# The low part of each group's second U block made by GpSimd between its row gathers, in the last phase of a PEER expert layer

## The reference, cut to what matters

```
def expert_block(args):
    xb, eb, gb = args
    h = jnp.einsum('td,ted->te', xb.astype(f32), u[eb].astype(f32))
    a = jax.nn.gelu(h, approximate=False) * gb
    return jnp.einsum('te,ted->td', a, v[eb].astype(f32))
```

## Time and profile before

| what | value |
|---|---|
| median of 3 runs | 3098.43 us |
| lowest and highest run | 3095.93 and 3102.11 us |
| span of the profiled execution | 3101.7 us |
| TensorE busy in it | 85% of the span |
| VectorE busy in it | 74% of the span |
| GpSimd busy in it | 52% of the span |

### The profile page before, as it was taken

One profiled execution on the slowest core, in us unless ns is written; L12 is line 12 of the kernel. 1 busy time (PEld: TensorE's weight loads), 2 busy tenths in 40 slices (PEclk: granted clock), 3 DMA queues, 4 the chain that ended last, 5 costly groups with the idle time before them and its releaser, 6 DMA issues.

```text
span 3101.7 us, 40708 instructions
## 1 busy us (share of the span) xinstructions
PE 2646.0 (85%) x14892; PEld 2060.6 (66%) x14892; DVE 2307.6 (74%) x4892; ACT 1052.2 (34%) x1650; POOL 1611.6 (52%) x1187
## 2 busy tenths in 40 slices
PE   7998688889997566663667999999999999999996
PEld 5888577777776455551445767777777777777775
DVE  4520666655999899983767778887777777879999
ACT  4321433433454577760112222222222322222322
POOL 0001001112887555564666666766666767666674
PEclk9988799999998788886888999999999999999998
DMA  4231412221210599999999999999999999999995
GB/s 130 95 103 56 141 44 86 86 83 62 76 52 29 173 320 296 298 322 346 383 390 385 381 391 382 396 393 394 387 395 365 396 407 409 394 394 345 367 377 213
DMA packets 309647, 832.90 MB, mean 269 GB/s; under 512 B 26096, under 2 KB 114608, under 8 KB 309456
## 3 DMA queue, kind: packets, MB, share of 16 engines
q0 software_dynamic: 150864, 548.60, 46.1%
q1 hardware_dynamic: 158592, 281.78, 25.6%
HBM read 771.40 MB, written 58.88 MB: 268 GB/s over the span
## 4 chain that ended last, share of the span: by engine, by line
PE 15%; DVE 13%; DMA 11%; POOL 9%; issue 6%; ACT 0%; DVEq 0%; ACTq 0%; POOLq 0%
DMA e_u_row<-in_u,ids 11%; POOL hold L1975 6%; DVE e_u_row L2213 3%; POOL e_u_row L1966 3%; PE psum L2051 2%; PE psum L2052 2%; PE psum L2053 2%; PE psum L2018 2%; PE psum L2019 2%; PE psum L2020 2%; PE psum L2066 2%; DVE e_y L2203 2%; DVE e_u_row L2222 1%; DVE e_vl L2171 1%; DVE hold L2222 1%
## 5 line engine op out<-in xcount | busy, mean ns | idle before, releaser
L1966 POOL DMA_INDIRECT e_u_row<-in_u,ids x384 | 484.4, 1261 | 339.0 <-DVE ids L2213 234.7
L2213 DVE CUSTOM_DVE_ANT_0 e_u_row<-e_u_row,hold 128x1024 f32<-128x1024 f32 x384 | 467.9, 1223 | 255.5 <-DMA e_u_row<-in_u,ids 228.4
L2051 PE MATMUL psum<-e_vh,e_ah 128*128 128x512 f32 x1024 | 421.5, 412 | 98.1 <-DVE e_y L2203 78.5
L1975 POOL DMA_INDIRECT hold<-in_v,ids x376 | 436.4, 1161 | 131.4 <-issue 109.2
L2052 PE MATMUL psum<-e_vl,e_ah 128*128 128x512 f32 x1024 | 410.1, 401 | 0.0
L2053 PE MATMUL psum<-e_vh,e_al 128*128 128x512 f32 x1024 | 407.9, 398 | 0.0
L2018 PE MATMUL psum<-x1d,e_uh 128*128 128x512 f32 x864 | 341.3, 395 | 0.0
L2019 PE MATMUL psum<-x1d,e_uh 128*128 128x512 f32 x864 | 337.3, 390 | 0.0
L2020 PE MATMUL psum<-x1d,e_ul 128*128 128x512 f32 x864 | 336.3, 389 | 0.0
L2051 PEld LDWEIGHTS psum<-e_vh,e_ah 128*128 128x128 f32 x1024 | 198.1, 193 | 204.0 <-DVE e_y L2203 103.7
L2203 DVE TENSOR_TENSOR e_y<-e_y,psum 128x512 f32<-128x512 f32 x464 | 298.9, 679 | 10.4 <-PE psum L2053 9.2
(11 more groups left out here) (406 smaller groups left out, 5673.1 us busy)
## 6 DMA issues: line engine op xcount, KB each, us to landing
e_vr<-in_v SPq DMA_DIRECT2D x128, 512.0 KB
e_ur<-in_uT SPq DMA_DIRECT2D x108, 512.0 KB
s_G<-g_tile SPq DMA_DIRECT2D x8, 4096.0 KB, 26.5
e_g<-s_G SPq DMA_DIRECT2D x64, 512.0 KB
ids<-in_w_ch SPq DMA_DIRECT2D x17, 512.0 KB, 4.1
s_ch<-p_out POOLq DMA_DIRECT2D x16, 512.0 KB, 4.4
hold<-in_wq SPq DMA_DIRECT2D x16, 512.0 KB, 8.9
hold<-in_v,ids POOLq DMA_INDIRECT x476
```

The lines of the kernel that those rows point to most:

```text
L1966: pool.indirect_dma_start(out=u_ring[n % U_RING][:], out_offset=None, in_=io["u"], in_offset=bass.IndirectOffsetOnAxis(ap=id_u[:, s, k:k + ...
L1975: pool.indirect_dma_start(out=v_ring[m % V_RING], out_offset=None, in_=io["v"], in_offset=bass.IndirectOffsetOnAxis(ap=id_v[:, t:t + 1], a ...
L2051: nc.tensor.matmul(acc, ah[s][j][:, r], vh[s][j][:, c], start=(first and j == 0), stop=False)
L2213: nc.vector.tensor_tensor_reduce(row, row, xs[:, s, :], 1.0, 0.0, ALU.mult, ALU.add, hs[:, s, k:k + 1]).then_inc(dotted, 1)
```

## The change

In groups 53 to 62 the subtraction that makes `e_ul1` for the next group, `split_u(g + 1, 1)`, is taken out of DVE's order. GpSimd does the same subtraction, on the same buffers and with the same semaphores, at places between its gathers: before the first gather that waits for a row of slot 4 or later of group g. That makes ten subtractions, for groups 54 to 63. The block for j = 0 stays on DVE, as do both blocks in the phases before.

```
+                def split_u_low(g):
+                    pool.wait_ge(u_hi[1], g - SHORT + 1)
+                    nc.gpsimd.tensor_tensor(ul[1][:], ur[1][:], uh[1][:].bitcast(F32), ALU.subtract).then_inc(u_lo[1], 1)
+
+                s_at = {n: g + c / U_SLOTS for (g, c), ns in sums.items() for n in ns}
+                split_next = KEEP + 1
                 for n in range(U_RING - 1, P):
+                    while split_next < NG and n >= S_RING and s_at[n - S_RING] >= split_next - 0.5:
+                        split_u_low(split_next)
+                        split_next += 1
                     gather_last(n)
+                for g in range(split_next, NG):
+                    split_u_low(g)
...
                     dot_rows(g, 5)
-                    if SHORT <= g + 1 < NG:
+                    if SHORT <= g + 1 <= KEEP:
                         split_u(g + 1, 1)
```

## The result

The changed kernel takes 3104.94 us (median of 14 runs, 3098.98 to 3118.0), the kernel before 3098.47 us beside it (14 runs). The ratio is 1.0029, with a 95% interval of 1.0019 to 1.0040: 9 us slower, 6 to 12. The ratio is not that of the two medians, which lie 6.5 us apart, inside this interval. The profiled execution took 3103.53 us, with a span of 3101.9.

What follows compares the result with a forecast made beforehand. DVE, without idle time in the last phase, was taken as the bound; 4 x 1.03 - 0.23 + 5 x 0.67 = +7.2 us on 3098.4 gave 3105.6 us, with 80% between 3099 and 3111.5.

Steps and rivals of the forecast that it cites:

- What bounds the kernel: Last phase: DVE is busy 25.00 of 25.00 us, so removing ten subtraction slots of 1.14 us saves 11.4 us.
- The exclusion: POOL operations reading SBUF and DVE operations with two SBUF operands exclude each other for their whole length, about 2.3 us.
- The two deductions: Amounts taken off DVE's stall behind POOL's subtraction: 0.13 us at `split_a`, 0.19 us at a sum.
- POOL works beside DVE: Rival, last phase: DVE only loses its ten slots, -11.4 us, or 3087.0; chance 0.07.
- The size of the stall: Last phase: each POOL subtraction costs DVE 2.3 us, less what falls beside a PSUM addition, less 0.13 to 0.19.
- The groups with two rows in slot 4: Groups 53 to 57: POOL gets through ahead of `split_a`, DVE loses 2.17 us, net +1.03 in four of them.
- Group 53: Two PSUM additions in a row there; the stall behind them was put at 0.91 us, net -0.23.
- the five groups with one row: Groups 58 to 62: POOL starts at the PSUM addition (+0.37) or before a sum (+0.97); middle +0.67 each.
- The Trainium skill's floor: POOL's subtraction at about 2.5 cycles per two-input element, 2.13 us; by it the forecast would be 3103.9.
- Only beside the additions from PSUM: Rival, last phase: POOL gets through only beside PSUM additions, +3.1 us, or 3101.5; chance 0.28.
- What the stall makes late next: Last phase: PE's idle time in a group grows, while DVE stays at 25.00 of 25.
- What costs nothing: Last phase: POOL's low part is ready at W + 5.3 to 5.9 against W + 6.6; the ring covers later gathers.

Runs made afterwards that it cites:

- eight columns: Changed kernel, but POOL subtracts only the first 8 of 1024 columns at the same place, leaving part of the result out; 3087.53 us, ratio 0.9967.
- copy on top: Kernel before, DVE keeping its subtractions, plus POOL copies of a 128x1024 block into a spare buffer at the changed kernel's places; 3102.95 us, ratio 1.0019.
- pairs alone: Kernel before, with DVE's four additions from PSUM made as two pairs from group 54 on; 3098.06 us, ratio 0.9999.
- two halves: Changed kernel with additions from PSUM as two pairs and POOL's subtraction cut in two, each half beside a pair; 3096.87 us, ratio 1.0001.
- a half each: Against the changed kernel, POOL subtracts only 512 columns, beside a pair of PSUM additions; DVE does the rest in the old place; 3098.77 us, ratio 0.9997.
- fastest complete kernel: Changed kernel with POOL's subtraction halved beside paired PSUM additions, and SP loading gates ahead of `e_ur1` from group 53 on; 3095.02 us, ratio 0.9982.

## Why the prediction was right, and where it was not

The forecast was 3105.6 us, +7.2; measured were 3104.9 (+6.5 by the medians), +9.0 by the ratio (6 to 12), and +9.7 in the profiled phase.

- **What bounds the kernel**: right. Eleven microseconds taken from DVE come out as 10 (eight columns).
- **The exclusion**: right, and shown from both sides: the same work on top of everything costs 18 us of lengthened rows, the same place without the work costs nothing. The two deductions, 0.13 and 0.19 us, hold to 0.01 us in the rows above. The rival that POOL works beside DVE is refuted.
- **The size of the stall**: the term was a little too large. Forecast were 18.6 us of stall (7.2 and the 11.4 saved); the ten rows lose 16.9. The groups with two rows in slot 4 were taken for 2.17 each behind `split_a`; of those four it was so in two (2.14), and in two POOL got through only at the addition (1.54). Group 53 lost 0.95 (0.91 forecast), the five groups with one row 1.58 to 1.93 (1.81). POOL's length is 2.39 us where it is let through at once, as the earlier trace rows had it. The Trainium skill's floor (GPSIMD Engine Reference, Instruction dispatch), by which I had estimated 2.13, is 0.26 below that.
- **Only beside the additions from PSUM**: this rival describes eight of the ten groups, but not its price of +3.1. It has 14.5 us of stall where 16.9 were lost: two groups lose at `split_a`, and in two more POOL starts 0.3 us after the addition and the sum loses 1.9. And it has no late gelu.
- **What the stall makes late next**: this step failed. The prediction had TensorE idle for longer, at no price, and DVE at 25.00 of 25.00. Instead a stall ahead of an addition from PSUM stops TensorE, in three groups its clock falls, gelu is late there, and DVE stands idle for 3.5 us more than before in the phase. In the two groups with the same stall and the same wait of TensorE gelu is late only where the clock fell. The length of TensorE's waits does not order the rest: in "copy on top" it waits 21.6 us for DVE's additions and DVE 1.2 for gelu, in "eight columns" 9.0 and 2.3. But leaving out "eight columns" and the wait at the phase's start, every wait for gelu of over 0.4 us in these kernels (17) ends 6 to 10 us behind the end of a stretch at the lower clock. Not every such stretch makes gelu late: the kernel before has one and no late gelu, "pairs alone" four and one late gelu. For the other two waits of the changed kernel (0.69 and 1.71 us), where TensorE also stood still for longer (5.51 and 3.65 us), the shares of the clock and of the stop stay open.
- **What costs nothing**: right for the changed kernel; there DVE waits neither for rows nor for gates. The margin is small, as two halves and a half each show, where a later signal makes the gates late.

The too large stall (1.7 us) and the missing terms, the wait for gelu (3.5 us) and 0.8 us lost in other sums and splits, partly cancel, so that the total is nearer than its terms is in part luck.

## What to carry to other kernels

Before work goes from VectorE to GpSimd, look at what VectorE does at that moment: beside instructions with two SBUF operands the work costs VectorE nearly its whole length on GpSimd, which here was twice the time it took on VectorE itself; beside instructions with one operand in PSUM it was free. Such places can be made by putting the PSUM instructions together, and the work can be cut to their length; then the signal that the moved work gives comes later, and the queue behind it has to be looked through, as SP's was here. The length of a stall, even on an engine without idle time, need not be its whole price: here TensorE waited for what stood behind it, and in some groups ran at the lower clock afterwards.

## What was not expected of the hardware

- TensorE's granted clock was 0.59 in a window of 5 us after it had stood still for 5.5 us, a stall of 2.14 us on VectorE on top of a wait that it has without it (3.25 us in the kernel before, with 0.66 behind it). But of two waits of 1.86 and 1.90 us only the second had a lower clock behind it (1.00 and 0.66).
- POOL released by `split_a` of DVE starts 0.22 us after DVE's next row has started; released by ACT earlier, it started with that row.
- In the fastest complete kernel 23 of the 128 sums take 1.30 to 1.33 us instead of 1.27, and each of them has a gather on POOL that starts 0.05 to 0.08 us after it. The 15 that have a gather within 0.02 us of their start keep 1.27 to 1.29. 19 more, all of them beside a half of the subtraction, take 1.38 to 1.49; all others keep their 1.27. So a gather that starts shortly after such a VectorE instruction costs it up to 0.06 us; why one that starts with it does not, the rows do not show.
